# Second feed-forward part of a two-layer diffusion block: down projections as seven block products chained in PSUM, with transfers that add into x

## The reference

```python
def swiglu(h, w_gate, w_up, w_down):
    return (jax.nn.silu(h @ w_gate) * (h @ w_up)) @ w_down
...
    x = x + g2 * swiglu(modulate(rmsnorm(x, norm_ffn[i]), sh2, sc2),
                        ffn_w_gate[i], ffn_w_up[i], ffn_w_down[i])
return rmsnorm(x, final_norm)
```

## Time and profile before

| | |
|---|---|
| median of three runs | 2331.09 us |
| the profiled execution: time / span of its instructions | 2330.7 / 2329.4 us |
| TensorE matmul busy, instructions | 2304.8 us (99%), 10989 |
| TensorE weight loads busy | 1907.7 us (82%) |
| VectorE, ScalarE, GpSimd busy | 1698.0 (73%), 803.9 (35%), 118.7 us (5%) |
| granted TensorE clock, mean | 0.999 of full speed |
| transfers: mean rate, issued by | 70 GB/s, SP alone |

### The profile page before, as it was taken

The page is one execution under the profiler, slowest core; times in us unless marked ns, Lnnn a source line. Parts: engine busy times, 40 slices in busy tenths (PEclk is TensorE's granted clock), DMA queues, the critical chain, the costliest instruction groups (busy, mean ns, idle before and its releaser), DMA issues.

```text
span 2329.4 us, 29137 instructions
## 1 busy us (share of the span) xinstructions
PE 2304.8 (99%) x10989; PEld 1907.7 (82%) x10989; DVE 1698.0 (73%) x2552; ACT 803.9 (35%) x1293; POOL 118.7 (5%) x90
## 2 busy tenths in 40 slices
PE   8999999999999999999999999999999999999998
PEld 5888888888888888888888788888888888888887
DVE  5777887886598888888886764264897777777777
ACT  6355555552443222222223411111532222222224
POOL 0101101000300000000001200001200000000002
PEclk9999999999999999999999999999999999999999
DMA  7101111132112333333322021121011111111112
GB/s 300 35 27 52 52 43 43 43 129 93 42 37 73 109 109 109 109 109 109 109 91 91 19 73 37 36 73 36 37 51 50 55 46 46 54 49 51 55 37 90
DMA packets 51960, 163.36 MB, mean 70 GB/s; under 512 B 7552, under 2 KB 12032, under 8 KB 51712
## 3 DMA queue, kind: packets, MB, share of 16 engines
q1 hardware_dynamic: 51840, 161.72, 20.7%
HBM read 157.51 MB, written 4.19 MB: 69 GB/s over the span
## 4 chain that ended last, share of the span: by engine, by line
PE 94%; DVE 4%; DMA 1%; ACT 1%; issue 0%; SPq 0%; POOL 0%; DVEq 0%; POOLq 0%; ACTq 0%
PE ps L635 26%; PE ps L637 26%; PE ps L636 26%; PE ps L1132 3%; PE ps L1066 2%; PE ps L1070 1%; PE ps L1068 1%; PE ps L1067 1%; PE ps L1071 1%; PE ps L1111 1%; PE ps L1113 1%; PE ps L1112 1%; DMA ada_ring<-ada_pe 1%; PE ps L902 1%; PE ps L911 0%
## 5 line engine op out<-in xcount | busy, mean ns | idle before, releaser
L2248 DVE SCALAR_TENSOR_TENSOR x<-ps,mods,x 128x512 f32<-128x512 f32 x440 | 322.7, 749 | 146.0 <-PE ps L637 126.7
L635 PE MATMUL ps<-g_hi,w_hi 128*128 128x512 f32 (+1 forms) x848 | 327.5, 386 | 0.1
L637 PE MATMUL ps<-g_hi,w_lo 128*128 128x512 f32 (+1 forms) x848 | 326.5, 385 | 0.0
L636 PE MATMUL ps<-g_lo,w_hi 128*128 128x512 f32 (+1 forms) x848 | 326.5, 385 | 0.0
L635 PE MATMUL ps<-h_hi,op_hi 128*128 128x512 f32 x640 | 249.2, 389 | 0.0
L637 PE MATMUL ps<-h_hi,op_lo 128*128 128x512 f32 x640 | 249.0, 389 | 0.0
L1779 ACT CAST op_hi<-rq 128x512 fp32r<-128x512 f32 x240 | 147.2, 623 | 234.1 <-PE ps L637 228.9
L1790 ACT ACTIVATE g_full<-g_full 128x512 f32<-128x512 f32 x80 | 50.8, 634 | 490.8 <-DVE g_full L2601 490.8
L635 PE MATMUL ps<-h_hi,w_hi 128*128 128x512 f32 x512 | 200.6, 392 | 1.6 <-DVE h_lo L2479 1.5
L637 PE MATMUL ps<-h_hi,w_lo 128*128 128x512 f32 x512 | 199.3, 389 | 0.0
L636 PE MATMUL ps<-h_lo,w_hi 128*128 128x512 f32 x512 | 199.3, 389 | 0.0
(11 more groups left out here) (365 smaller groups left out, 4492.0 us busy)
## 6 DMA issues: line engine op xcount, KB each, us to landing
rq<-stream SPq DMA_DIRECT2D x80, 512.0 KB, 3.6
mod_raw_f<-ada_rows SPq DMA_DIRECT2D x48, 512.0 KB, 3.5
raw<-stream SPq DMA_DIRECT2D x46, 512.0 KB, 3.6
w_lo_f<-stream SPq DMA_DIRECT2D x46, 512.0 KB, 4.4
mod_raw<-ada_rows SPq DMA_DIRECT2D x32, 512.0 KB, 3.5
ada_ring<-ada_pe SPq DMA_DIRECT2D x16, 512.0 KB, 11.3
x<-x_t SPq DMA_DIRECT2D x8, 512.0 KB, 7.3
x0a<-x_t SPq DMA_DIRECT2D x2, 1024.0 KB, 6.2
```

Of the source, the lines that this page charges most:

```text
L635: nc.tensor.matmul(out, w[0][wi], a[0][ai], start=start, stop=False)
L636: nc.tensor.matmul(out, w[0][wi], a[1][ai], start=False, stop=False)
L637: return nc.tensor.matmul(out, w[1][wi], a[0][ai], start=False, stop=stop)
L2248: nc.vector.scalar_tensor_tensor(out=x[:, m, HALF[half]], in0=ps[:, out_bank(d, m), :], scalar=mods[:, gate + m:gate + m + 1], in1=x[:, m, ...
```

## The change

In the ten blocks of the second feed-forward part (now `duo_block`; the first feed-forward part is left as it was):

- The down projection of a pair is also made by seven block products (P1 to P7, 4 output tiles x 3 passes = 12 matmuls each, 84 in place of 96), for pairs 0 to 8. They go through the same operand ring and stand between the gate and up products, in every third place (`DUO`); the last pair's down projection is made plainly as before (`down_end_duo`, `down_last`).
- Products are chained in PSUM: S2 is accumulated onto A11, S3 onto that, A22 onto that (`CHAIN`), and S1, S4 onto A12. So a product starts only when the sum before it has been read: `keep` (ScalarE, copies the bank for A11, S2, S3) and `corner_part` (VectorE, adds the bank to the copy). The same with the down products: P6, P7, P4 are accumulated onto P1, and P3 onto P5; each of the 7 x 4 intermediate sums is added to a quarter of x.
- Of these 28 evictions a block, 12 (after P7, P2, P3) are VectorE's as before (`near_out`); 16 (after P1, P6, P4, P5) are ScalarE's (`far_out`: far = ps * gate, four buffers), and a transfer issued by GpSimd adds each far buffer (128 x 512 float32, 256 KB) to x (`accum_op=ALU.add`).
- VectorE makes the sums of the down weights (`down_sum`) and of the corners (`pair_diff`); corners and sums lie in pairs of buffers (`pair_full`, `pair_op`, places K, X0 to Y2), split by ScalarE (`pair_split`) and VectorE (`pair_lower`). The raw down weights now go to `w_hi_f` directly.
- The eight loads of x count on one semaphore, and the first eviction to x waits for all of them.

```diff
+DOWN = 2
+DUO_FIRST = tuple((mat, name) for mat in (GATE, UP) for name in ("A11", "A12")) \
+    + tuple((mat, name) for name in ("S2", "S3", "S1", "S4", "A22") for mat in (GATE, UP))
+DUO = ((GATE, "A11"), (UP, "A11"), (DOWN, "P1"), (GATE, "A12"), (UP, "A12"), (DOWN, "P6"), (GATE, "S2"), (UP, "S2"),
+       (DOWN, "P7"), (GATE, "S3"), (UP, "S3"), (DOWN, "P4"), (GATE, "S1"), (UP, "S1"), (DOWN, "P2"), (GATE, "S4"),
+       (UP, "S4"), (DOWN, "P5"), (GATE, "A22"), (UP, "A22"), (DOWN, "P3"))
+DUO_LAST = ((GATE, "A11"), (UP, "A11"), (DOWN, "P1"), (GATE, "A12"), (UP, "A12"), (DOWN, "P6"), (GATE, "S2"),
+            (DOWN, "P7"), (UP, "S2"), (DOWN, "P4"), (GATE, "S3"), (DOWN, "P2"), (UP, "S3"), (DOWN, "P5"), (GATE, "A22"),
+            (DOWN, "P3"), (UP, "A22"), (GATE, "S1"), (UP, "S1"), (GATE, "S4"), (UP, "S4"))
+DUO_END = WINO - 1
+DUO_RING = [(n, key) for n in range(WINO) for key in (DUO_FIRST if n == 0 else DUO_LAST if n == DUO_END else DUO)]
+DUO_AT = {at: N_PROD * WINO + n for n, at in enumerate(DUO_RING)}
...
+DOWNS = ("P1", "P6", "P7", "P4", "P2", "P5", "P3")
+DOWN_B = {"P1": "C11", "P6": "T2", "P7": "T3", "P4": "T4", "P2": "C21", "P5": "C12", "P3": "C22"}
+DOWN_X = {"P1": (0, A), "P6": (0, B), "P7": (4, B), "P4": (4, A), "P2": (0, A), "P5": (4, B), "P3": (0, B)}
+CHAIN = ("A11", "S2", "S3", "A22")
+FAR = ("P1", "P6", "P4", "P5")
+NEAR = ("P7", "P2", "P3")
...
+FAR = ("P1", "P6", "P4", "P5")
+NEAR = ("P7", "P2", "P3")
+KEPT = ("A11", "S2", "S3")
...
+    def ring_free(eng, at):
+        was = at - 4 - N_PROD * WINO
+        if was < 0:
+            eng.wait_ge(prod, at - 3)
+            return
+        n, key = DUO_RING[was]
+        if key[0] == DOWN:
+            eng.wait_ge(down_p, down_pd(n, key[1]))
+        else:
+            eng.wait_ge(prod, DUO_PROD[n, key])
...
+    def mm3(out, w, wi, a, ai, start, stop, more=False):
+        nc.tensor.matmul(out, w[0][wi], a[0][ai], start=start and not more, stop=False, skip_group_check=more)
+        nc.tensor.matmul(out, w[0][wi], a[1][ai], start=False, stop=False, skip_group_check=more)
+        return nc.tensor.matmul(out, w[1][wi], a[0][ai], start=False, stop=stop, skip_group_check=more)
...
-            sp.dma_start(x[:, k, :], x_view[:, k, :]).then_inc(in_x[k], 16)
+            sp.dma_start(x[:, k, :], x_view[:, k, :]).then_inc(in_x, 16)
...
+        def down_raw_in(n):
+            at, dst = f1_at(6 * (n + 1) + 4), w_lo_f if n == DUO_END else w_hi_f
+            for f in range(2):
+                sp.dma_start(dst[:, 4 + f, :], stream[at + f]).then_inc(in_dn[f], 16)
...
+        def bank_read_duo(n, mat, name):
+            if name in ("S2", "S3", "A22"):
+                pe.wait_ge(kept, kept_n(n, mat, CHAIN[CHAIN.index(name) - 1]))
+            elif name in ("S1", "S4"):
+                pe.wait_ge(corner_in, read_at(n, "C11" if name == "S1" else "C22", mat))
...
+        def duo_product(n, mat, name, job=None):
+            at = DUO_AT[n, (mat, name)]
+            pe.wait_ge(op_l, at + 1)
+            if mat == DOWN:
+                what = DOWN_B[name]
+                pe.wait_ge(pair_low, low_n(n - 1, what))
+                for m in range(4):
+                    down_read(pe, n, name, m)
+                    mm3(ps[:, 4 + m, :], (op_hi, op_lo), (ALL, at % 4, slice(m * P, (m + 1) * P)),
+                        pair_op[home(n - 1, what)], ALL, True, True, name not in ("P1", "P2", "P5")).then_inc(down_p, 1)
+                return
+            bank_read_duo(n, mat, name)
+            if n == 0 and name in ("S2", "S3", "S1", "A22"):
+                pe.wait_ge(b_l, 4 + ("S2", "S3", "S1", "A22").index(name) + 1)
+            out, more = ps[:, duo_bank(mat, name), :], name not in ("A11", "A12", "S1")
+            for k in range(KH):
+                last = mm3(out, (op_hi, op_lo), (ALL, at % 4, slice(k * P, (k + 1) * P)), operand_b[WINO_B[name]],
+                           (ALL, k, ALL), k == 0, k == KH - 1, more)
+                if k == 0 and job is not None:
+                    job_sum(job)
+            last.then_inc(prod, 1)
+        def down_end_duo():
...
+            for key in DUO_LAST[:18]:
+                duo_product(n, *key)
+            pe.wait_ge(dn_l, 2 * WINO + 2)
+            down_end_duo()
+            duo_product(n, UP, "S1")
+            duo_product(n, GATE, "S4")
+            job_sum(job_a)
+            duo_product(n, UP, "S4")
+            job_bcast(job_a)
+            down_last(D_END + 1)
...
+        def keep(n, mat, name):
+            act.wait_ge(prod, DUO_PROD[n, (mat, name)])
+            if n > 0:
+                act.wait_ge(down_p, down_pd(n, {"A11": "P1", "S2": "P6", "S3": "P7"}[name]))
+            place = home(n, {"A11": "C11", "S2": "C12", "S3": "C22"}[name])
+            copy(pair_full[place][mat][:], ps[:, duo_bank(mat, name), :]).then_inc(kept, 1)
...
+        def far_out(n, name):
+            for m in range(4):
+                at = far_n(n, name, m)
+                act.wait_ge(down_p, down_pd(n, name) - 3 + m)
+                if at >= 4:
+                    act.wait_ge(far_in[at % 4], 16 * (at // 4))
+                row = DOWN_X[name][0] + m
+                nc.scalar.mul(far[at % 4][:], ps[:, 4 + m, :], mods[:, GATES[3] + row:GATES[3] + row + 1])\
+                    .then_inc(far_set, 1)
+        def duo_first():
+            keep(0, GATE, "A11")
...
+        def duo_first():
+            keep(0, GATE, "A11")
+            duo_tops(0, 4, 6)
+            b_top("f1", "T1")
+            pair_gate(0, "C11")
+            keep(0, UP, "A11")
+            duo_tops(0, 6, 8)
+            pair_split(0, "C11")
+            for n, (name, mat) in enumerate((("S2", GATE), ("S2", UP), ("S3", GATE), ("S3", UP))):
+                keep(0, mat, name)
+                duo_tops(0, n + 8, n + 9)
+            b_top("f1", "T4")
+            duo_tops(0, 12, 13)
...
+            duo_tops(n, 3, 4)
+            pair_split(n - 1, "T4", True)
+            duo_tops(n, 4, 6)
+            far_out(n, "P1")
+            keep(n, GATE, "A11")
+            keep(n, UP, "A11")
+            duo_tops(n, 6, 8)
+            pair_gate(n, "C11")
+            far_out(n, "P6")
...
+        def down_sum(n, name):
+            a11, a21 = w_hi_f[:, 4, 0:HT], w_hi_f[:, 4, HT:D]
+            a12, a22 = w_hi_f[:, 5, 0:HT], w_hi_f[:, 5, HT:D]
+            if name == "P5":
+                for f in range(2):
+                    dve.wait_ge(in_dn[f], 16 * (WINO + n))
+                ins = nc.vector.tensor_tensor(a21, a21, a22, ALU.add)
+            elif name == "P6":
+                dve.wait_ge(w_sum, w_sum_n(n, "P5"))
+                ins = nc.vector.tensor_tensor(a11, a21, a11, ALU.subtract)
+            elif name == "P7":
+                dve.wait_ge(w_sum, w_sum_n(n, "P6"))
+                ring_free(dve, DUO_AT[n, (DOWN, "P7")])
+                ins = nc.vector.tensor_tensor(duo_src(n, DOWN, "P7"), a22, a11, ALU.subtract)
+            else:
+                ins = nc.vector.tensor_tensor(a12, a12, a11, ALU.subtract)
+            ins.then_inc(w_sum, 1)
...
+        def near_out(n, name, gate):
+            first, half = DOWN_X[name]
+            for m in range(4):
+                dve.wait_ge(down_p, down_pd(n, name) - 3 + m)
+                if name != "P7":
+                    far_landed(dve, n, {"P2": "P1", "P3": "P6"}[name], m)
+                elif n > 1:
+                    far_landed(dve, n - 1, "P5", m)
+                row = first + m
+                nc.vector.scalar_tensor_tensor(out=x[:, row, HALF[half]], in0=ps[:, 4 + m, :],
+                                               scalar=mods[:, gate + row:gate + row + 1], in1=x[:, row, HALF[half]],
+                                               op0=ALU.mult, op1=ALU.add).then_inc(xe, 1)
+        def duo_first(gate):
...
+        def duo_first(gate):
+            b_part("f1", "T4")
+            to_x(D_F1, 0, gate)
+            to_x(D_F1, 1, gate)
+            ffn_inner("f1", 0, 3)
+            to_x(D_F1, 2, gate)
+            to_x(D_F1, 3, gate)
+            b_low("f1", "T2")
+            duo_sums(0, GATE)
+            b_low("f1", "T3")
+            duo_lows(0, 4, 5)
+            duo_sums(0, UP)
+            duo_lows(0, 5, 6)
+            corner_part(0, "C11", GATE)
+            for m in range(4, KD):
+                to_x(D_F1, m, gate)
+            corner_part(0, "C11", UP)
+            duo_lows(0, 6, 7)
+            pair_mult(0, "C11")
+            duo_lows(0, 7, 9)
+            b_low("f1", "T1")
...
+        for n in range(1, WINO):
+            for name in FAR:
+                for m in range(4):
+                    at = far_n(n, name, m)
+                    row, half = DOWN_X[name][0] + m, DOWN_X[name][1]
+                    if name == "P5":
+                        pool.wait_ge(xe, near_xe(n, "P7", m))
+                    elif n == 1:
+                        pool.wait_ge(xe, xe_at(D_F1 + half, row))
+                    elif name == "P4":
+                        far_landed(pool, n - 1, "P4", m)
```

(6 more changed lines are left out.)

519 lines of the change are left out of this document (473 added, 46 removed).

## The result

The changed kernel takes **2311.01 us** (median of four runs, 2310.86 to 2312.05) against 2331.27 us for the kernel before beside it: ratio 0.9913, 95% interval 0.9896 to 0.993, 20.3 us less. Forecast: 2309.0 us, 22 us less. The profiled execution has a span of 2309.7 us (before 2329.4).

The account below looks back on a forecast made before the run. TensorE's matmuls were taken to bound the phase, 0.2267 us each. -24.5 + 1.1 + 1.3 = -22.1 us on the profiled 2330.7 gave 2308.6, or 2309.0 us as median; range 2305.5 to 2320, about 0.8.

Parts of the forecast that it names:

- The matmuls: Nine pairs made with 84 in place of 96 down matmuls: 108 fewer at 0.2267 us each, -24.5 us.
- Middle blocks without a wait: Middle blocks, 252 matmuls in 57.1 us: every operand and copy comes in time, so TensorE's waits are put at 0.
- P7's margin: Middle block, tightest place found: P7's operand is ready at 19.2 us and needed at 21.8, margin given as 2.5 us.
- the cadence sum of 40.4: VectorE per middle block: 54 instructions at 0.60 us plus 12 evictions at 0.67, together 40.4 of 57.1 us.
- The first block: TensorE waits on ScalarE's copies of up's A11 (1.1 us) and gate's S2 (1.3 us), together +2.4 us.
- The adding transfers: GpSimd-issued transfers adding far buffers to x: landing taken as 2.1 us, one at a time, costing 0.
- the budget: P1's far buffers must be empty when ScalarE evicts P6: 11 us for one transfer, or 3.3 us each one by one.
- The rival of their pace: Adding transfers finish only one by one and set the block's length; slower above 3.74 us each, about 2425 at 4.4; chance 0.10.
- GpSimd's work stretching VectorE: Rival: each transfer issue lengthens a VectorE two-SBUF-input instruction by 1.03 us; 14 us in all, about 2323; chance 0.07.
- Tight queues: Rival: slower crossings between engines use up P7's 2.5 us; about 1 us a block, 9 more, 2318; chance 0.09.
- x's eight loads: First eviction to x waits for all eight loads; idle VectorE behind it covers up to about 3 us; priced 0.
- The tail: Last pair and final norm keep their order, awaited transfers issued over 15 us earlier: 0, give or take 1 us.

Follow-up runs that it names:

- the second profile: The changed kernel run again unedited, beside the run with four edits: 2311.83 us, ratio 0.9914 to the kernel before.

## Why the prediction was right, and where it was short

- **The matmuls**: -24.5 us by 57.12 us a block, confirmed.
- **Middle blocks without a wait**: confirmed, with less room than the working had, and in that some luck. The slower landing of the weights beside the adding transfers (6.3 us, taken 4.4) had no term: P7's margin is 1.8 us in the block looked at, 1.0 in the tightest and 0.7 in the second profile, where I had 2.5; and VectorE's busy time is 42.2 us a block, not 46 (I added single durations, but the records overlap; the cadence sum of 40.4 was the better guide). ScalarE has 30.6 us against a sum of 29.4.
- **The first block**: both places, their cause and their size came out: 2.46 us against 2.4, the copies ending at 1718.0 and 1722.1 against 1718.0 and 1722.0. The first is shown by its removal. The second copy would have held TensorE alone, as the first stop had made S3's rest come in time; with that stop gone, 0.7 us are S3's rest's, which the walk left out.
- **The step that was short** is that the sum has no wait outside the front of the first block. I walked a middle block and the front of the first, not the two seams. At the end of the first block the chain has no P3 to hide behind (1.1 us). In the last block I looked at P7's operand, one place earlier, and not at P4, chained onto P7 and only one product behind it (1.4 us, 0.5 to 0.6 when the weights land earlier). The idle time in brackets is 4.0 us in all, where I had called for 2 to 3. Two stops of 2.5 us together were missed, and 0.6 us too little was credited, as the old stop for T1's rest went under the new ones. That is the difference of 2 us between -22.1 and -20.0.
- **The adding transfers**: their price was wrong by a factor of two (4.4 us, taken 2.1) and the term of 0 right, as the budget was 11 us. By the Trainium skill ("DMA: Bandwidth & Descriptors", section on the anatomy of one DMA by the gpsimd path) it would be an estimated 2.6 us; the trace disagrees, with 3.3 us at least. The rival of their pace doesn't hold: four landings overlap. What it had right is that they can bind, by buffers times landing, as two buffers show.
- **GpSimd's work stretching VectorE**: not with issues, but with additions, by 1.09 us an instruction. By the Trainium skill ("SBUF — State Buffer", section on the two separate sides) a VectorE instruction with two SBUF inputs is blocked only by a GpSimd instruction that reads SBUF; both runs agree (0.69 us beside issues, 1.78 beside additions).
- **Tight queues**: no wait at this block length, though only 1.0 and 0.7 us from one in the tightest blocks; right 2.4 us below it.
- **x's eight loads**: the first eviction to x now starts at 528.01 us, behind a wait of 0.62 on the loads, and VectorE idles 2.50 us behind it: covered, as argued from the earlier trace rows.
- **The tail, 0 give or take 1**: no step of the change acts there, but the size of its scatter was too small (below).

## What to carry to other kernels

When work is chained and queues are in order, walk the first and the last round of a loop as well as a middle one: the middle had no wait, and all the loss lay in the first and the last block, half of it where a product that hides a chain is missing. A transfer off the path still costs in two ways, by the buffers that wait for its landing and by the loads that it slows, so count buffers against landing time and reread the landing of every load beside it, in the worst block and not in the median alone. And measure a gain of a few microseconds on a stretch between two fixed instructions, since the ends of the program scatter by as much.
